# Moving the pooled means from VectorE to GpSimd and tightening the pace of a depthwise convolution

## The reference

```python
y_conf = conformer_conv(conf_ab, ...)          # gate, 31-tap causal depthwise conv, layer norm, silu, 256x256 matmul
y_att  = forgetting_attention(q, k, v, f)      # 4 heads, 4 query blocks of 128 tokens each
y_sc   = short_conv_mixer(sc_h, sc_b, sc_c)    # 3-tap conv between two gates
y_pool = multiscale_pool(pool_v, w_pool, s)    # below
mix = jnp.concatenate([y_conf, y_att, y_sc, y_pool], axis=-1) @ w_out
```

## Time and profile before

| | |
|---|---|
| median of 3 runs | 1494.48 us (1494.46 to 1496.58) |
| profiled execution, its own time | 1495.4 us |
| its span in the trace | 1493.6 us |
| PE busy | 98% of the span |
| DVE, ACT, POOL busy | 54%, 38%, 17% of the span |
| granted PE clock, mean | 0.989 |

### The profile page before, as it was taken

One profiled execution on the slowest core, in us unless ns is written; L12 is line 12 of the kernel. 1 busy time (PEld: TensorE's weight loads), 2 busy tenths in 40 slices (PEclk: granted clock), 3 DMA queues, 4 the chain that ended last, 5 costly groups with the idle time before them and its releaser, 6 DMA issues.

```text
span 1493.6 us, 17745 instructions
## 1 busy us (share of the span) xinstructions
PE 1460.6 (98%) x6978; PEld 1192.0 (80%) x6978; DVE 809.7 (54%) x1167; ACT 560.6 (38%) x829; POOL 254.2 (17%) x170
## 2 busy tenths in 40 slices
PE   9999989999999999899999999999999999999998
PEld 7866768888888887677789887788887888888887
DVE  5688465433333357574678734634535665534564
ACT  5345434523323125433355545322224443323310
POOL 4234344301101013340033203100003000000000
PEclk9999999999999999998999999999999999999999
DMA  6221222432333332211211111333332233232331
GB/s 228 88 68 57 71 71 71 121 105 85 101 97 99 99 96 74 85 57 57 71 43 58 51 35 43 113 94 93 96 102 82 74 113 110 87 111 85 99 100 69
DMA packets 36131, 129.18 MB, mean 86 GB/s; under 512 B 4024, under 2 KB 4280, under 8 KB 36048
## 3 DMA queue, kind: packets, MB, share of 16 engines
q1 hardware_dynamic: 35760, 127.78, 27.7%
q10 hardware_dynamic: 288, 0.26, 0.1%
HBM read 125.91 MB, written 2.10 MB: 86 GB/s over the span
## 4 chain that ended last, share of the span: by engine, by line
PE 86%; DVE 6%; ACT 2%; POOL 2%; issue 2%; DMA 0%; ACTq 0%; POOLq 0%; DVEq 0%
PE P L1073 25%; PE P L1075 25%; PE P L1074 25%; PE P L1332 1%; PE P L1114 1%; DVE P L1886 1%; POOL AC L2363 1%; PE P L1115 1%; PE P L1116 1%; PE P L1218 1%; DVE WL L1732 1%; POOL H L2372 1%; PE P L1294 1%; PE P L1169 1%; POOL DD L2363 1%
## 5 line engine op out<-in xcount | busy, mean ns | idle before, releaser
L1073 PE MATMUL P<-AH,WH 128*128 128x512 f32 x1104 | 445.5, 404 | 8.9 <-issue 4.4
L1074 PE MATMUL P<-AL,WH 128*128 128x512 f32 x1104 | 434.3, 393 | 0.0
L1075 PE MATMUL P<-AH,WL 128*128 128x512 f32 x1104 | 434.3, 393 | 0.0
L1412 ACT ACTIVATE WH<-WR 128x1024 fp32r<-128x1024 f32 x232 | 243.8, 1051 | 337.0 <-PE P L1075 321.6
L1732 DVE TENSOR_TENSOR WL<-WR,WH 128x1024 fp32r<-128x1024 f32 x215 | 279.0, 1298 | 158.8 <-ACT WH L1412 158.3
L1073 PEld LDWEIGHTS P<-AH,WH 128*128 128x128 f32 x1104 | 210.1, 190 | 62.8 <-issue 14.2
L1075 PEld LDWEIGHTS P<-AH,WL 128*128 128x128 f32 x1104 | 209.8, 190 | 45.0
L1074 PEld LDWEIGHTS P<-AL,WH 128*128 128x128 f32 x1104 | 210.1, 190 | 42.4 <-issue 0.7
L1075 PE MATMUL P<-FH,WL 128*128 128x512 f32 x432 | 168.1, 389 | 0.0
L1073 PE MATMUL P<-FH,WH 128*128 128x512 f32 x432 | 168.1, 389 | 0.0
L1074 PE MATMUL P<-FL,WH 128*128 128x512 f32 x432 | 168.1, 389 | 0.0
(11 more groups left out here) (320 smaller groups left out, 1873.8 us busy)
## 6 DMA issues: line engine op xcount, KB each, us to landing
WR<-in_ws SPq DMA_DIRECT2D x232, 512.0 KB, 3.6
out<-Y SPq DMA_DIRECT2D x8, 256.0 KB, 2.0
H<-in_xT SPq DMA_DIRECT2D x3, 512.0 KB, 8.2
C<-in_const SPq DMA_DIRECT2D x1, 946.5 KB, 11.1
H<-in_xT SPq DMA_DIRECT2D x2, 256.0 KB, 4.1
PR<-in_pT SPq DMA_DIRECT2D x1, 512.0 KB, 4.6
WR<-in_ws SPq DMA_DIRECT2D x1, 384.0 KB, 4.4
WR<-in_ws ACTq DMA_DIRECT2D x1, 128.0 KB, 3.8
```

The costliest lines, as they stand in the source:

```text
L1073: e.matmul(P, wh, xh, start=start, stop=False)
L1074: e.matmul(P, wh, xl, start=False, stop=False)
L1075: ins = e.matmul(P, wl, xh, start=False, stop=stop)
L1412: e.activation(m.WH[:, c % NW, :], m.WR[:, c % NRAW, :], ACT.Copy).then_inc(*at.up("w_hi", "w_hi", c))
```

## The change

The diff has two parts.

The first moves `pool_means` from DVE's program to POOL's. Before, DVE ran six instructions for each j: for each half of the partitions one that multiplies the window sum by 1/w and subtracts the feature (L1934, 64x512), and two on the first 16 tokens (L1938, L1941). After, POOL runs five: for each half a multiplication by 1/w (64x512) and a correction of the first 16 tokens (64x16), and then one subtraction over all 128 partitions (128x512). The places in the order (blocks 95 and 132) are the same, and so are ACT's and DVE's other functions of these steps.

The second says taps 17 to 30 of the convolution's tile 1 at every block, so tap 18 is said at block 145, 19 at 146, 20 at 147, 21 at 148 and tap 30 at 157. All later steps of `conformer` move seven blocks up: `ln_mean` to 158, `ln_center` to 160, `ln_var` to 165, `ln_out` to 170, and the two small tiles to block 176, inside the last tile of part 0.

```diff
@@ conformer
-                yield 1 + tap % 2
+                yield 1 if j and tap > 16 else 1 + tap % 2
@@ vector_program: removed, also from its table `run`
-    def pool_means(j):
-        D = m.DD[:, j, :]
-        w.wait_ge(*at("pool_sums", j))
-        if j:
-            w.wait_ge(*at("warmed"))
-        for g in range(2):
-            rows = slice(64 * g, 64 * g + 64)
-            sm = (m.S2, m.S4)[g][rows, 16:16 + T]
-            a = CONST_COLS["inv"][0] + j
-            e.scalar_tensor_tensor(D[rows, :], sm, m.C[rows, a:a + 1], m.PV[rows, 16:16 + T], ALU.mult,
-                                   ALU.subtract).then_inc(*at.up("pool_means", "pool_mean", j, g))
-            w.wait_ge(*at("pool_mean", j, g))
-            a = CONST_COLS["warm"][0] + 16 * j
-            e.tensor_tensor(D[rows, 0:16], sm[:, 0:16], m.C[rows, a:a + 16], ALU.mult).then_inc(
-                *at.up("pool_means", "pool_first", j, g))
-            w.wait_ge(*at("pool_first", j, g))
-            e.tensor_tensor(D[rows, 0:16], D[rows, 0:16], m.PV[rows, 16:32], ALU.subtract).then_inc(
-                *at.up("pool_means", "pool_means", j))
@@ gpsimd_program: added, also to its table `run`
+    def pool_means(j):
+        D = m.DD[:, j, :]
+        w.wait_ge(*at("const"))
+        if j:
+            w.wait_ge(*at("warmed"))
+        for g in range(2):
+            rows = slice(64 * g, 64 * g + 64)
+            sm = (m.S2, m.S4)[g][rows, 16:16 + T]
+            a = CONST_COLS["inv"][0] + j
+            turn()
+            e.tensor_scalar(D[rows, :], sm, m.C[rows, a:a + 1], None, ALU.mult).then_inc(
+                *at.up("pool_mean", "pool_mean", j, g))
+            did("pool_mean", j, g)
+            a = CONST_COLS["warm"][0] + 16 * j
+            turn()
+            e.tensor_tensor(D[rows, 0:16], sm[:, 0:16], m.C[rows, a:a + 16], ALU.mult).then_inc(
+                *at.up("pool_mean", "pool_first", j, g))
+            did("pool_first", j, g)
+        turn()
+        e.tensor_tensor(D, D, m.PV[:, 16:16 + T], ALU.subtract).then_inc(*at.up("pool_means", "pool_means", j))
+        did("pool_means", j)
```

More of the change, by code:

```diff
@@ L2322, in vector_program @@
            "split1": split1, "glu_gate": glu_gate, "glu": glu, "dwconv": dwconv, "ln_mean": ln_mean,
-           "ln_center": ln_center, "ln_var": ln_var, "ln_out": ln_out, "pool_in": pool_in, "pool_means": pool_means,
+           "ln_center": ln_center, "ln_var": ln_var, "ln_out": ln_out, "pool_in": pool_in,
            "pool_lo": pool_lo, "sc_c": sc_c, "sc_h": sc_h, "sc_b": sc_b, "mix1": mix1, "ple_in": ple_in, "up1": up1,
@@ L2498, in gpsimd_program @@
     run = {"w_lo_pool": w_lo_pool, "square": square, "residual": residual, "clear1": clear1, "glu_gate": glu_gate,
-           "pool_sums": pool_sums, "sc_c": sc_c, "sc_h": sc_h, "ple_in": ple_in, "up1": up1, "lv_clear": lv_clear,
+           "pool_sums": pool_sums, "pool_means": pool_means, "sc_c": sc_c, "sc_h": sc_h, "ple_in": ple_in, "up1": up1, "lv_clear": lv_clear,
            "lv_ref": lv_ref, "lv_scale": lv_scale, "st_scale0": st_scale0, "gn_square": gn_square, "gn_out": gn_out,
```

## The result

| | before | changed |
|---|---|---|
| median | 1495.53 us (4 runs, 1494.46 to 1498.43) | 1509.55 us (4 runs, 1504.62 to 1513.92) |
| profiled execution | 1495.4 us, span 1493.6 | 1504.62 us, span 1502.8 |
| ratio | | 1.0092, 95% interval 1.0064 to 1.0121 |

The forecast was 1497.7 us with a range up to 1500.8. The sign was right; the rise over the median of before is 14.0 us where 3.2 was forecast, and even the fastest run lies above the range. Here are the page's rows of busy time and of the chain after, against the earlier trace rows. Busy times hardly moved, so the loss is not added work; POOL's share of the chain that ended last went from 2% to 4%.

The account below looks back on a forecast made before the run. PE, busy 98% of the span, was taken to bound the kernel, so only its waits could change. Terms 1.4 + 1.25 + 1.35 - 0.6 = +3.4 us, taken as +3.2, gave 1497.7 us, range 1495.3 to 1500.8.

Parts of the forecast that it names:

- The start of the means, and who waits: POOL starts j = 0 at 83.54; ACT waits for it; PE's waits at unit 1 and `values1(10)` grow, unit 12's goes.
- The length of the means: POOL's five instructions of one j take 3.4 us, ends 2.7 and 5.1, with 0.70 us per one-operand product.
- d: Time of POOL's five means instructions for one j, gaps included: 3.4 us, ends 2.7 and 5.1.
- the two terms, d - 2.0 and d - 2.15: Longer PE waits: +1.4 us at unit 1's transposes (j = 0), +1.25 us at `values1(10)` (j = 1).
- Rival A: POOL is slow: one-operand product costs 1.06 to 1.28 us, d is 4.1 to 4.6, time 1499.6 us; chance 0.20.
- The estimate of 0.55 us: One-operand product on POOL by the Trainium skill's page: some 0.55 us, which would make d 3.1 us.
- the scaling and PE's transposes follow at the distances of before: For j = 0, behind the later DH, PE restarts at 88.06; its wait of 1.07 us becomes 2.5 us.
- The taps: From block 145, extra taps on DVE delay the mask of unit 15 and so `values1(14)`: +1.35 us, ends 0.7 and 1.6.
- `ln_mean` finds the last tap within 0.2 us of need, behind the column sums of tile 0: `ln_mean`, said seven blocks earlier, finds the convolution's last tap within 0.2 us of need, behind tile 0's column sums.
- The small tiles: At the branch's end PE no longer waits for a late-copied PSUM bank, only for CLl: -0.6 us, ends 0 and -1.6.
- The relief of VectorE: DVE loses 3.03 us (j = 0) and about 3.9 us (j = 1) of means; its queueing beside POOL goes: real but hidden.
- Rival C: Faster: waits of 1.07 and 1.2 us and the small tile's 0.6 vanish if DH comes before 84.4: 1491.6 us; chance 0.05.

Follow-up runs that it names:

- means_late: Changed kernel with the old tap pace, ScalarE's high part its own step nine or six blocks behind the means: 1492.27 us, ratio 0.9985 to before.
- stall_5: Kernel before, with ScalarE writing DH of j = 0 five more times ahead of the probabilities: 1501.48 us, ratio 1.0045.
- stall_2: Kernel before, with ScalarE writing DH of j = 0 two more times ahead of the probabilities: 1497.66 us, ratio 1.0015.
- late_pace22_gap: `means_late` with tile 1's taps at every block from tap 22, column sums three blocks behind the last tap: 1492.16 us, ratio 0.9984 to before.

## Why the prediction was wrong

**The start of the means, and who waits.** Right. GpSimd began at 83.69 for a forecast of 83.54, ACT stood in its own `pool_means`, PE's wait for unit 1 grew, the scores of unit 12 no longer waited, and the wait moved to `values1(10)`.

**The length of the means.** This is the first term that was mis-sized. I took 0.70 us for the one-operand product because the time seemed to go with the operands streamed; it takes 1.56 us, and d is 5.17 us, beyond even the outer end of 5.1. The other guesses held: 0.21 to 0.22 us for the 16 columns (taken 0.15), 1.26 for the subtraction (1.28), 0.1 for the gaps. With d = 5.17 the two terms, d - 2.0 and d - 2.15, are 3.2 and 3.0 instead of 1.4 and 1.25. The longest waits, 4.31 for 1.07 and 4.44 for 1.2, grew by about that, 3.24 each. Rival A had the direction, but its dearest product was 1.28 us. That bound was itself a misreading: I had called SC's 1.28 us the slowest ordinary group of this size, but in the same trace POOL's 33 two-operand instructions on AC and SQ (128x512) take 1.49 us each and its 13 on DD and SQ 1.62. With 1.62 the outer end of d would have been 5.7 us, and the measured 5.17 inside it. The rule of the Trainium skill (GPSIMD Engine Reference, When to use GPSIMD) that one-input work runs at about line rate on GpSimd is not borne out for this instruction: 1.56 us, or 1.49 with an immediate, for 512 columns, where its two-input work took 1.03. The page's advice to leave elementwise work on VectorE would have been the better guide for the change as made, though not for `means_late`. The estimate of 0.55 us that the prediction gives by that page has no working beside it, and the measured time is nearly three times as long.

**What a wait costs.** This is the step that failed: "the scaling and PE's transposes follow at the distances of before". They follow at half the clock. Behind the waits of 4.31 and 4.44 us PE lost 3.4 and about 2.7 us more, and `stall_5` shows that the wait alone does it. The forecast had no term for the clock. It lacked one even for d = 3.4, since the wait of 2.41 us in `stall_2` lost 1.7 us of clock in its profiled execution. Such a price stood in the trace of the kernel before, outside the stretch that I read. Two long waits in its timeline of PE, and the windows behind them:

```profile
579.12 0.47 PE L1073 MATMUL P<-AH,WH 128*128 128x512 f32 x1 [2.13 <-ACT AH L1426]
603.34 1.22 PE L1169 MATMUL P<-C,AC 128*128 128x1 f32 x8 [3.29 <-POOL AC L2363]
```

```profile
580.00:584.00 4.00, 4.00 (x13) 3.10 (x12) 3.83 (x4) 1.82 (x3) 2.53 (x2) 0.57 0.00 0
604.00:608.00 4.00, 4.00 (x14) 3.25 (x14) 3.00 (x13) 0.00 (x0) 0.00 (x0) 0.57 0.00 0
```

Each misses 4 x 0.43 = 1.7 us. A term of up to 1.7 us for each of the two forecast waits of 2.5 us could have been taken from here, as an estimate. That puts 1497.7 at 1501.1 us, still too low, because d was too small as well.

**The taps.** The term of +1.35 us at `values1(14)` came out as 0.38 at the block that needs the pooled branch's low part (L1856, which now has one more tap ahead of it) and 0.67 at `values1(14)`, 1.05 in all: right in kind. "`ln_mean` finds the last tap within 0.2 us of need, behind the column sums of tile 0" was wrong. The step first waits until bank 6 is free, which is when the last tap has read it, so the sums of tile 0 cover nothing, and PE waits 0.6 us. Behind it the clock falls (1.7 us). The pace as a whole was forecast at +0.75 us and measured at +1.8 (-0.3 to +4.0).

**The small tiles.** Forecast -0.6 us, the wait fell from 1.66 to 1.23: right.

**The relief of VectorE.** I called its gain real but hidden. It is worth 2.2 us as soon as ScalarE doesn't stand in front of it (`means_late`). Rival C was right in its mechanism and in its condition, which the change as made doesn't meet.

**The sum by measured parts.** Waits of the means 4.31 + 4.44 - 1.07 - 1.2 = +6.5; clock behind them 3.4 + 2.7 = 6.1; the pace 1.05 + 0.6 - 0.45 = +1.2 in waits and 1.7 in clock. That is 15.5 us, for a median 14.0 above before's; what is left over lies within the interval of the ratio (9.6 to 18.1 us).

## What to carry to other kernels

Before work moves to another engine, look at who stands in line for its result. The move pays only if the consumer's step moves too, and here the same five GpSimd instructions cost 10 us or gained 2 by that alone. On a kernel in which PE is 98% busy, add a term for the clock to a new wait of PE: in these traces nothing behind waits of up to 1.8 us in this stage (unless column sums followed), 1.7 us behind one of 1.87 further on, 0 or 1.7 us behind those of 2.1 to 2.4, 1.7 or 3.4 behind those of 3.2 to 3.4, and 3.4 at those of 4.1 to 4.5. Read the price from the windows behind the long waits that the kernel already has, and count only what falls after PE is back. And a step that is moved up to the edge of its input is not free because it waits little: check what follows the wait.

## What the runs showed of the hardware that was not expected

A GpSimd tensor_scalar over 64x512 fp32 took 1.56 us with the scalar from memory and 1.49 with an immediate, a tensor_tensor over the same data 1.03 us. So for this product the two-operand form with a broadcast column is the cheaper one by a third.

The granted clock of PE fell to half at waits of 4.3, 3.2 and 2.4 us, for 6.9, 6.8 and about 3.5 us, and part of that can lie before PE is back. The same wait of 2.13 us lost clock in nine traces and none in five. It also fell behind a wait of 0.6 or 0.9 us followed by 1.95 us of matmuls of a single column, and did not where the same matmuls had no wait ahead (clock 1.00 from 156 to 164 in `late_pace22_gap`). A wait is not the only cause: in the kernel before it also fell behind eight matmuls of 16 rows (4.93 us from 693.91, no idle time ahead), and 3.4 us are missing there from 696 to 708.

The time of one kernel varies with it: the 32 runs of the kernel before beside the second group of experiments reach from 1489.41 us at a clock of 0.993 to 1497.16 at 0.987.
